# A new front for a two-layer hybrid decoder step: statistics from token rows, the gate product tile by tile, and cached samples in phases of 13 slots

## What is computed

```python
hp = rmsnorm(x_prompt, norm_mix[0]); hs = rmsnorm(x_sample, norm_mix[0])
q, k, v, f = split(h @ w_qkvf, [D, 2*D, 3*D])        # f: one gate per head
logf = log_sigmoid(f + b_f); cum = cumsum(logf)
s = (q . k) / 8 + cum_q - cum_k                       # masked, softmax, times v
# prompt: its own k, v; samples: cache_k, cache_v, cache_logf by page, and the new row
```

## Time and profile before

| | |
|---|---|
| median of 3 runs | 2832.23 us (2828.47 to 2838.03) |
| profiled execution: time, span | 2835.53 us, 2833.6 us |
| PE busy | 2698.9 us, 95% of the span |
| DVE, ACT, POOL busy | 1076.5, 890.4, 1124.5 us (38%, 31%, 40%) |
| memory traffic | 290.53 MB, mean 103 GB/s |

### The profile page before, as it was taken

How to read it: one execution, slowest core, us unless ns; L and a number is a source line. 1 busy time by engine, 2 the same in 40 slices (tenths; PEclk the granted TensorE clock), 3 DMA queues, 4 the chain that set the end, 5 groups by cost and what they waited for, 6 DMA issues and landing times.

```text
span 2833.6 us, 44077 instructions
## 1 busy us (share of the span) xinstructions
PE 2698.9 (95%) x17527; PEld 2482.8 (88%) x17527; DVE 1076.5 (38%) x1236; ACT 890.4 (31%) x1535; POOL 1124.5 (40%) x490
## 2 busy tenths in 40 slices
PE   6969999999879999999999999999999999999997
PEld 4546766666569999999999999999999999999997
DVE  6756666766542321221222243333232122122224
ACT  4146666666653321111111141111232111111123
POOL 5376566666305333233333362222433333233334
PEclk8989999999889999999999999999999999999999
DMA  6666777776571111111111111111111111111112
GB/s 233 216 203 230 258 261 252 240 240 235 174 240 56 46 40 50 45 41 55 45 37 52 41 56 46 45 44 44 46 45 39 55 47 37 52 46 42 54 34 79
DMA packets 287260, 290.53 MB, mean 103 GB/s; under 512 B 11475, under 2 KB 249044, under 8 KB 287014
## 3 DMA queue, kind: packets, MB, share of 16 engines
q1 hardware_dynamic: 265730, 275.25, 30.3%
q10 hardware_dynamic: 21268, 12.63, 1.4%
q0 software_dynamic: 144, 1.05, 0.1%
HBM read 267.65 MB, written 21.28 MB: 102 GB/s over the span
## 4 chain that ended last, share of the span: by engine, by line
PE 81%; POOL 6%; DMA 4%; DVE 4%; ACT 2%; issue 1%; SPq 1%; ACTq 0%; DVEq 0%; POOLq 0%
PE PS L1182 69%; POOL kpage L645 4%; DMA vpage<-in_cache_v 2%; PE PS L1356 2%; DMA kpage<-in_cache_k 2%; PE PS L1298 2%; PE PS L1396 1%; PE PS L1333 1%; PE PS L1398 1%; PE PS L1397 1%; PE PS L1370 1%; PE PS L1372 1%; ACT probs L859 1%; DVE nmax L1779 1%; POOL raw L654 1%
## 5 line engine op out<-in xcount | busy, mean ns | idle before, releaser
L605 POOL TENSOR_TENSOR w_lo<-raw,w_hi 128x1024 fp32r<-128x1024 f32 (+1 forms) x193 | 463.1, 2399 | 1205.9 <-ACT w_hi L779 1205.9
L779 ACT ACTIVATE w_hi<-raw 128x1024 fp32r<-128x1024 f32 (+1 forms) x193 | 204.1, 1057 | 1258.5 <-PE PS L1182 1246.2
L1182 PE MATMUL PS<-a_hi,w_hi 128*128 128x344 f32 x2712 | 576.3, 321 | 5.5 <-DVE xf L1612 4.5
L1182 PE MATMUL PS<-a_lo,w_hi 128*128 128x344 f32 x2712 | 575.9, 321 | 0.0
L1182 PE MATMUL PS<-a_hi,w_lo 128*128 128x344 f32 x2712 | 573.0, 320 | 0.0
L1591 DVE SCALAR_TENSOR_TENSOR t<-PS,rinv 128x1032 f32<-128x1032 f32 x112 | 138.0, 1233 | 876.1 <-PE PS L1182 874.5
L1182 PEld LDWEIGHTS PS<-a_hi,w_hi 128*128 128x128 f32 x2712 | 456.8, 188 | 5.9 <-DVE xf L1612 4.6
L1182 PEld LDWEIGHTS PS<-a_lo,w_hi 128*128 128x128 f32 x2712 | 459.4, 189 | 0.0
L1182 PEld LDWEIGHTS PS<-a_hi,w_lo 128*128 128x128 f32 x2712 | 452.2, 188 | 0.0
L645 POOL TENSOR_TENSOR kpage<-kpage,q_bc 128x1024 f32<-128x1024 f32 x128 | 303.6, 2386 | 198.1 <-DMA kpage<-in_cache_k 166.5
L1182 PE MATMUL PS<-b_hi,w_hi 128*128 128x344 f32 x1440 | 308.4, 323 | 12.3 <-DVE b_lo L1943 12.2
(11 more groups left out here) (236 smaller groups left out, 2939.5 us busy)
## 6 DMA issues: line engine op xcount, KB each, us to landing
kpage<-in_cache_k SPq DMA_DIRECT2D x128, 512.0 KB, 4.5
vpage<-in_cache_v SPq DMA_DIRECT2D x128, 512.0 KB, 5.1
raw<-in_w_ffn_in SPq DMA_DIRECT2D x88, 512.0 KB, 3.8
wseg<-in_attn_w_qkvf SPq DMA_DIRECT2D x12, 1024.0 KB, 5.3
raw<-in_attn_w_qkvf SPq DMA_DIRECT2D x24, 512.0 KB, 4.4
raw<-in_w_ffn_out SPq DMA_DIRECT2D x32, 384.0 KB, 3.4
raw<-in_conv_w_in SPq DMA_DIRECT2D x24, 512.0 KB, 3.8
raw<-in_w_ffn_out SPq DMA_DIRECT2D x32, 320.0 KB, 3.1
```

The lines of the kernel that those rows point to most:

```text
L605: gp.tensor_tensor(w_lo[s][:, 0:kts, 0:cols], raw[s][:, 0:kts, 0:cols], w_hi[s][:, 0:kts, 0:cols].bitcast(F32), ALU.subtract).then_inc(w_l ...
L779: act.activation(w_hi[s][:, :, 0:cols], raw[s][:, :, 0:cols], ACT.Copy).then_inc(w_hid[s], 1)
L1182: ins = pe.matmul(g[:, b, :], w[:, k, :], x[:, k, b * TB:(b + 1) * TB], start=k == 0 and n == 0, stop=k == kts - 1 and n == 2)
```

## The change

The front is rewritten and the samples are shifted against the pairs:

- **Tiles.** PE multiplies the gate columns of tile k as soon as its `a_lo` is there (`gate_step`), and turns tile k+2 behind it (`turn_x`). Tiles have 1024 columns. The squares come from token rows on ACT, two rows per tile from tile 4 on, with their sums accumulated on the way; POOL adds nothing up. The factors 1/rms are spread over the partitions by one pair of matmuls with a diagonal (`diag`).
- **Gates.** The log-sigmoid works on 128 partitions × 144 elements instead of 16 × 1032, and is spread between the halves of pair 0's projection, as are the scans and the turned biases.
- **Samples.** Their projections q, k and v come as 24 pages of 128 × 1024 weights through the buffers of the value pages, each in four quadrants at once (`proj_page`). The 8 pages of q are taken in the front, the 16 of k and v in slots 0 to 10 of pair 0. The input rows of the samples are loaded four times, into each quadrant (`xs4`).
- **Loop.** Slots are counted through from 0 to 119. Sample b starts in slot 14+13b; `KEYS` and `VALS` say in which of its 13 slots its pages come. Four key pages of sample 0 stay in the front, 12 move into pair 0. The new row's scores are made in slots 5 to 9 of pair 0.
- **Buffers.** They are laid out so that POOL, ACT and SP need no common `ready`.
- **Gone.** The 12 segments, the squares on POOL, and the 16 key pages ahead of the loop.

The core of the diff:

```diff
-    PRODUCT_SLOT = [4, 5, 6, 6, 7, 8, 8, 9, 10, 10, 11, 12, 12, 13, 13, 14]
-    KEY_SLOT = [1, 2, 2, 3, 3, 4, 4, 5, 6, 7, 8, 9, 10, 11, 12, 13]
+    BASE, PACE = 14, 13
+    KEYS = [1, 2, 2, 3, 4, 5, 5, 6, 7, 8, 8, 9, 10, 11, 11, 12]
+    VALS = [4, 5, 5, 6, 6, 7, 7, 8, 8, 9, 9, 10, 10, 11, 11, 12]
+    FRONT_KEYS = 4
+    KEY_AT = [-1] * FRONT_KEYS + list(range(NPG - FRONT_KEYS)) + [BASE + PACE * (b - 1) + g for b in range(1, NSEQ) for g in KEYS]
+    NPROJ = 3 * KT
+    VAL_AT = [-1] * KT + [0, 0, 1, 2, 2, 3, 4, 4] + [6, 7, 7, 8, 9, 9, 10, 10]
+    VAL_AT += [BASE + PACE * b + g for b in range(NSEQ) for g in VALS]
...
+            act.wait_ge(wf_in, 16)
+            act.activation(w_hi[0][:, :, 0:H], wf[:, :, :], ACT.Copy).then_inc(w_hid[0], 1)
+            act.wait_ge(vec_d, 1)
+            for m in range(KT):
+                act.wait_ge(fev, fe.up())
+                g = vecs[:, m, NORMS["mix0"]:NORMS["mix0"] + 1]
+                act.activation(a_hi[:, m, 0:S], xf[m % 3][:, :], ACT.Copy, scale=g).then_inc(ahi, 1)
+                act.dma_start(x_spill[m, :, 0:S], xf[m % 3][:, :]).then_inc(xsp[m % 3], 16)
...
+            def gate_step(k):
+                pe.wait_ge(alo, k + 1)
+                for n, (w, x) in enumerate(((w_hi[0], a_hi), (w_hi[0], a_lo), (w_lo[0], a_hi))):
+                    for b in range(2):
+                        ins = pe.matmul(bank(6 + b), w[:, k, :], x[:, k, b * BANK:(b + 1) * BANK],
+                                        start=k == 0 and n == 0, stop=k == KT - 1 and n == 2)
...
+            for k in range(KT):
+                gate_step(k)
+                if k + 2 < KT:
+                    turn_x(k + 2)
+                if k >= 3:
+                    proj_page(k - 3)
+            for m in range(5, KT):
+                proj_page(m)
...
-                    if n == 1:
-                        sample_max(i)
-                    if n == 3:
-                        sample_spread(i)
+                    b, r = phase(i, n)
+                    if r == 0 and b > 0:
+                        sample_turn(b - 1)
+                    if r == 3 and b >= 0:
+                        sample_spread(b)
...
+            project(0, 0, 0, 4)
+            pe.wait_ge(gzc, 1)
+            for t in range(TT):
+                ins = pe.transpose(bank(0, P + t * H, P + (t + 1) * H), gz[:, t * P:(t + 1) * P], ident[0:H, 0:H])
+            ins.then_inc(ztt, 1)
+            project(0, 0, 4, 8)
+            pe.wait_ge(dgd, 1)
...
+            project(0, 1)
+            pe.wait_ge(ltd, 1)
...
+            project(1, 0)
+            pe.wait_ge(lct, 1)
...
+            project(1, 1)
+            turn_pages(0)
+            turn_pages(1)
+            project(2, 0)
+            turn_pages(2)
+            turn_pages(3)
+            project(2, 1)
```

More of the change, by code:

```diff
@@ L616, in add_squares @@
                 sums.up()
-            then(gp.memset(sqs0[:, :], 0.0))
-            then(gp.memset(w_lo[0][:, :, :].bitcast(F32), 0.0))
-            for m in range(KT):
-                add_squares(sqs0[:, :], sqt[m % 2][:, :], first=m == 0)
-                if m == 0:
-                    low(0, cols=H)
-            gp.wait_ge(ftr, KT)
-            gp.wait_ge(vec_t, 1)
-            gp.indirect_dma_start(out=lf[:, :], out_offset=None, in_=logf_pages,
-                                  in_offset=bass.IndirectOffsetOnAxis(ap=page_col[:, 0:1], axis=0)).then_inc(lf_in, 16)
             def low_q(n):
@@ L683, in pair, with multiply_for @@
-            def pair(i):
-                for g in range(NPG):
-                    if i < LAST:
-                        multiply((i + 1) * NPG + g)
-                    if g == 2 and i < LAST:
+            def multiply_for(slot):
+                for n in range(NPAGES):
+                    if KEY_AT[n] == slot:
+                        multiply(n)
+            multiply(0)
+            low_q(2)
+            multiply(1)
+            low_query(0)
+            multiply(2)
+            multiply(3)
@@ L701, in _ @@
+                    multiply_for(slot + 1)
             for i in range(NPAIR):
@@ L703, in _ @@
             wh[0].value, wh[1].value = w_count(3 * NPAIR - 1), w_count(3 * NPAIR - 2)
+            sq.value = sums.value = KT
             low(0)
@@ L1014, in pair @@
                 normalise(i, 3)
+                sample(9)
+                if i == 0:
+                    sample_new()
                 if i < LAST - 1:
@@ L1027, in pair @@
                 normalise(i, 1)
+                sample(11)
                 if more:
@@ L1704, in _ @@
-            then(dve.tensor_tensor(s_new[0:NSEQ, :, :], s_new[0:NSEQ, :, :], neg_b, ALU.add))
-            dve.wait_ge(lbe, 4)
-            dve.wait_ge(w_lod[0], 1)
-            dve.wait_ge(sqa, KT)
-            dve.wait_ge(out0, 64)
-            dve.wait_ge(qsp, 16)
-            dve.nop().then_inc(ready, 1)
-            dve.memset(bank(7), 1.0)
+                    dve.wait_ge(ahi, ah.up())
+                    dve.scalar_tensor_tensor(out=a_lo[:, m - 1, 0:S], in0=xf[(m - 1) % 3][:, :], scalar=vecs[:, m - 1, g:g + 1],
+                                             in1=a_hi[:, m - 1, 0:S].bitcast(F32), op0=ALU.mult, op1=ALU.subtract)\
+                       .then_inc(alo, 1)
@@ new lines, in _ @@
+            lc3 = lc[:, :].rearrange("p (r h) -> p h r", h=H)
+            for h in range(H):
+                ins = dve.tensor_tensor_scan(lc3[:, h, :], ones[:, 0:PAGE], lf3[:, h, :], 0.0, ALU.mult, ALU.add)
+            then(ins)
+            dve.tensor_copy(tot[:, :], lc[:, (PAGE - 1) * H:PAGE * H]).then_inc(lct, 1)
+            dve.memset(bank(7), 1.0).then_inc(b7d, 1)
+            dve.wait_ge(ncd, 2)
+            for q in range(2):
+                dve.scalar_tensor_tensor(out=negcum[32 + 64 * q:32 + 64 * q + H, :], in0=cum[:, :], scalar=-1.0,
+                                         in1=negcum[0:H, :].bitcast(F32), op0=ALU.mult, op1=ALU.subtract).then_inc(ncd, 1)
```

737 lines of the change are left out of this document (424 added, 313 removed).

## The result

The changed kernel takes **2840.1 us** (median of 20 runs, 2831.2 to 2847.7) against 2833.1 (20 runs): ratio 1.0024, 95% interval 1.0015 to 1.0033. It is slightly slower, by less than the 0.3% taken as the bound, where 2796 and "faster" were forecast. The profiled execution has a span of 2841.0 us, 7.4 more than before.

The account below looks back on a forecast made before the run. The loop was taken as bound by PE, the front by anything but PE. Front -49, extra pages +9 and `mdiag` waits +4 gave -36 us on 2835.5, 2799.5; 3.3 us off for the median made 2796, range 2776 to 2818.

Parts of the forecast that it names:

- Placing moves too: In the loop, value pages in other slots fill or miss PE's wait before slot 6: 0 us, between -3 and +4.
- misplaced pages add up: Rival: the loop's waits for misplaced pages cost 3 us in each of pairs 1 to 6, 2814 us; chance 0.08.
- a pair takes over 89 us: Sign in the loop that the forecast is wrong; pairs 1 to 6 were expected at 85 to 86 us.
- The front: Everything until pair 0 starts: start at 118 us against 166.9, 49 us earlier.
- The rings: Six serial rounds in the front of gate step, eight turns, copy and `a_lo`: 6.5 us each, 39 us together.
- gate weights: At the front's beginning, their load is issued at 12.6 us and their copy begins at 18.0.
- the projection of pair 0: In the front from 68.8 us: matmuls 33.4, turns and small products 6, PE's waits and handovers 7 us.
- DVE beside POOL: In the front, DVE's scans and small operations slow down while POOL works: 3 us, ends 0 and 8.
- the other waits and handovers: During pair 0's projection, PE's waits for late DVE, 2.6 and 1.3 us, plus 3 us for handovers: 7 us.
- Pair 0: First pair of the loop: k and v weight pages replace sample 0's value pages, so it stays as long.
- the extra pages: In pairs 1 to 7, sixteen more value pages at 0.58 us each: 9 us.
- mdiag: In the loop, PE waits for ACT's `mdiag` in about half of the samples: 4 us, between 0 and 16.

Follow-up runs that it names:

- v_wide: Changed kernel with each sample's sixteen value products spread over slots 4 to 14 instead of 4 to 12, sample end two slots later: 2808.9 us.
- v4_wide: Changed kernel with four value-page buffers instead of three and the value products spread over slots 4 to 14: 2786.0 us.
- v_once: Changed kernel without 125 of the 128 value-page loads, the products running over the same buffers as often as before: 2784.9 us.
- v_first: Changed kernel with value loads ahead of key loads in each of SP's slots: 2850.5 us.
- k_thin: Changed kernel loading only 64 of 1024 columns of every key page from the fourth on, with load order and waits kept: 2806.4 us.
- v4: Changed kernel with four value-page buffers instead of three, small tiles sharing memory to make room: 2803.2 us.
- v_mid: Changed kernel where, of two value pages in a slot, PE takes the first in mid-slot instead of both back to back: 2835.3 us.
- before_dense: Kernel before the change, at its 15 slots a sample, with value products in the changed kernel's slots 4 to 12: 2889.1 us.
- k_once: Changed kernel without 125 of the 128 key-page loads, POOL multiplying q_bc by itself instead: 2790.3 us.

## Why the prediction was wrong

- **The step that failed** is "Placing moves too: value pages no longer stand always in slots 4 to 14 ... I set 0, between -3 and +4". The rhythm of `VALS` was read as a matter of which gaps the pages fill. It also sets how long each buffer has for its next page. Both numbers for this stood in the text, landing 5.1 and a slot of 5.6 us, but only the keys were put through such a sum. The value: 31 to 37 us by spreading the pages alone (v_wide), 54 with a fourth buffer (v4_wide), where 0 was taken.
- **The rival "misplaced pages add up"** (0.08) had the right place and too small a size: 3 us a pair on top of the forecast 85 to 86, measured 8 in pairs 1 to 5. It had no mechanism, so no way to a size. The sign that was set for it, "a pair takes over 89 us", is what happened.
- **The front**: 49 us earlier forecast, 40.1 measured. The rings were right, (61.32 - 22.02)/6 = 6.55 us against 6.5; gate weights and first product came 1.2 us late, and the projection of pair 0 began at 71.2 instead of 68.8. From there to the turned keys it took 55.6 us instead of 49.2, and two terms were mis-sized. All steps were priced at the high clock, 33.4 + 6 = 39.4 us; PE was busy 45.0 us, at a granted clock of 0.89. And "DVE beside POOL" was taken as 3, with 8 as its end: scans and the copy of `tot` were held for 4.3 + 2.0 us on PE's path, 6.3, and the first step on `wt` beside a key page took 1.84 instead of the 0.24 of the next one. That PE's idle time came out at 10.5 us against 7 + 3 is luck: the other waits and handovers were 4, not 7. The Trainium skill, "SBUF — State Buffer", section "Who interferes with whom", gives by its rule 9.6 us in place of 3, and 124.6 for the start, measured 126.8. That is nearer, but as a price for this term it is as far above the 6.3 of the rows as 3 is below; what closes the sum is the clock (+5.6), beside +3.3 for this term, -3 for the other waits and +2.4 for the later begin. Its rule that an instruction is shut out for its whole length fits the rows: the copy of `tot` begins at 100.58 and ends at 102.74, and POOL's `q_lo` runs from 100.24 to 102.72.
- **Pair 0** was forecast at its old length and fell from 85.8 to 76.4. Its pages of weights cost about the same (8.8 us for sixteen), but PE waits 0.4 us in it where the pair before, with value pages and a clock of 0.97, lost 7.4 to idle time. By luck this balanced the front's shortfall: the start of pair 1 is 49.6 us earlier, as was forecast for pair 0.
- **Right**: the extra pages (13 of the 16 fall into pairs 1 to 5; v_once, at a clock of 0.99 as before, has 4.7 us more busy time than before, where 0.58 each would be 7.5); `mdiag`, 3.5 us measured over five pairs against 4; the keys, whose page waits on POOL fell from 166.5 to 106.7 in all; and the clock, which stayed at 0.73 in the rings, between the two levels weighed.

The rest of the sum comes out near without that table: v4_wide, which changes the slots of the value pages, their buffers and what ends a sample, took 2786 us, inside the range of 2776 to 2818 and 10 under the forecast of 2796. Its terms partly cancel: the front is 43.8 us shorter and not 49, pair 0 is 9.4 shorter and not as long, and pairs 1 to 5 are 6.1 longer.

## What to carry to other kernels

Where a table or schedule places the uses of a ring of buffers, work out for each use the time since the release of its buffer, and hold the shortest of these, not the mean rate, against issue plus landing in its slower cases. With two uses back to back in each slot over three buffers, every second use has one slot, and here one line of a table moved the time by 57 us at an unchanged rate. The number of pages per second said nothing: of the kernels that load all pages, the fastest moved the most per second.

When two streams share one queue and both hold buffers, reordering them can merely move the wait, as v_first showed here. Another buffer together with a wider spacing removed it.

## What the runs showed of the hardware

- A one-input copy on DVE is held up by POOL as well as the scans with two inputs: `tot`, 128x16, took 2.16 us instead of 0.17. This agrees with the Trainium skill, "SBUF — State Buffer", section "Who interferes with whom", which counts fast copies among the instructions that can need the port shared with GpSimd. POOL suffers too: one `w_lo` took 7.30 us beside sixteen scans instead of 2.38.
- Waits of 1 to 4 us in a loop that is otherwise full cost more than themselves. Over pairs 1 to 5 the changed kernel has 32.7 us more idle time of PE than v_once, which does the same products, and 18.0 us more busy time, at a granted clock of 0.95 instead of 0.99. So 1.55 us go with each us of waits. In the same comparison, (idle + busy) over idle, k_thin gives 1.5, v_first and v4 1.4, and v_mid, with more and shorter waits, 1.9; before_dense against before gives 1.3.
- Key traffic lengthens value landings by 0.8 us in the median, 5.3 against 4.5 (k_thin) and 4.4 (k_once). The slowest show no such order: 8.3 us with it, 6.3 in k_thin and 8.5 in k_once.
